# Forgetting attention: the output products of two heads issued together, alternating between the two column halves of the array

## The chip, the cores and the metric

The kernel runs on one core of a Trainium2 chip. The metric is the device time of one execution in microseconds (us), the median over several runs. TensorE (PE) multiplies, VectorE (DVE) and ScalarE (ACT) work on elements and move results out of the matmul banks (PSUM, banks of 128 partitions by 512 fp32 values), GpSimd (POOL) prepares weights, SyncE (SP) starts the loads. The engines run side by side, each in its own program order, and meet only at semaphores.

## The reference

Two blocks stand behind each other: a first block with a gated chunk mixer and a recurrent mixer, and a second with a feed-forward part, a hybrid mixer, a cross attention to a memory, and another feed-forward part. Sequence length is 512, width 1024, everything is fp32. The change touches the forgetting attention in the hybrid mixer:

```python
F = jnp.cumsum(jax.nn.log_sigmoid(f_logit.astype(jnp.float32)), axis=1).transpose(0, 2, 1)
...
s = jnp.einsum('bhqd,bshd->bhqs', q_blk, k, preferred_element_type=jnp.float32)
s = s + F_blk[..., None] - F[:, :, None, :]
s = jnp.where(pos_blk[:, None] >= k_pos[None, :], s, -jnp.inf)
p = jax.nn.softmax(s, axis=-1).astype(v.dtype)
return jnp.einsum('bhqs,bshd->bqhd', p, v)
```

There are 8 heads of 64 dimensions and 4 query tiles of 128 rows.

## The kernel before

**The stage.** The attention (`pe_fox`, `dve_fox`, `act_fox`, `pool_fox`) is a pipeline of `STEPS` = 32 steps: step i is head h = i // 4 and query tile qt = i % 4, and works on the first n = 128 (qt + 1) keys, since the attention is causal. Each engine has a loop over i that is unrolled in its own order. Beside the attention each step carries three of the 96 products of the convolution branch's projection (`pe_conv_products`: 9 matmuls of 128x512, L1679 to L1681), and that branch's elementwise work on DVE and ACT.

**One step on PE (iteration i).** First four matmuls that make the scores of step i (L1924 to L1927). Then the transposes of the softmax of step i - 2 (L1934, one for each key tile). Then, where a head begins (qt = 0) from i = 8 on, the output product `fox_out` of head h - 2 (L1953), so at i = 8, 12, 16, 20, 24, 28 and 32; the last head follows after the loop. Then the convolution products. After the 32 steps two more iterations (i = 32 and 33) carry the last transposes and 12 matmuls each of another projection (L1698 to L1700).

**The softmax.** For step i DVE takes the row maximum (L1978), ACT the exponential with its row sum (L2046), DVE the reciprocal (L1972), ACT multiplies by it (L2040, done in ACT's iteration i + 1). PE transposes the result (in its iteration i + 2), and ACT copies the transposed tile to SBUF (L2036, first thing in its iteration i + 3). ACT and DVE have other things in line between these: the taps of the convolution (L1719, up to three behind each other on DVE), L1709 that reads the projection's bank, L1737 and L1742 on ACT, and the preparation of the next head's queries, keys and rows (L1793, L1798, L1802 and L1816 on ACT, L1806 and L1810 on DVE).

**The output product.** The transposed softmax of a head lies in `FPT[:, h % 2]`, so there is a buffer for even heads and one for odd heads. `fox_out(pe, h)` waits for the four copies of head h (semaphore `fx_pt`) and makes four matmuls, one for each key tile, with 512, 384, 256 and 128 columns. The values of the head (128 keys by 64 dimensions) are the stationary operand. An even head writes partitions 0 to 63 of bank 4 and an odd head partitions 64 to 127; when both are there, ACT copies the bank (`act_fox_out`, L2070, semaphore `fx_oc`). ACT's first copy of a head h (step 4h) overwrites the buffer of head h - 2 and so waits for that head's output product (semaphore `fx_o`).

All operands of `fox_out` are plain fp32 (`FV` and `FPT`), and the trace has two matmul records for each such matmul of the program: 8 for a head, 64 for all.

Of the kernel before, what the change touches and what calls it, by code (L numbers as in the profile page):

```python
# [26 lines left out]
P = 128  # L27
SEQ = 512
TOK = SEQ // P
# [9 lines left out]
FOXH, FOXD = 8, 64  # L39
# [5 lines left out]
MH, MHD = 4, 256  # L45
# [89 lines left out]
def _members(kind, *parts):  # L135
# [21 lines left out]
    [("beta_tanh", 1), ("a_exp", 1), ("rows_exp", 1)],  # L157
    [("b_gates_lo", KB), ("causal", 2), ("masks", 26)], [("b_thg", KB), ("g_th", 4 * GH)], [("b_sg", KB), ("fx_r", FOXH * TOK)],
    [("raw_first0", 16), ("mem_in", 32)], [("raw_first1", 16), ("stored", 16 * KD)],
    [("fx_o", FOXH), ("ma_o", 2 * MH)], [("fx_hi", FOXH // 2), ("ma_hi", 2 * MH)], [("fx_lo", FOXH // 2), ("ma_lo", 2 * MH)],  # L160
]


class Sems:
# [18 lines left out]
    def due(self, name, value):  # L183

        return self(name), value + self.start.get(name, 0)
# [21 lines left out]
def build(nc, dram, out, phases=PHASES, dump=None):  # L207
# [3 lines left out]
    with ctx:  # L211
        base = 16640

        def place(name, at_kib, shape, dt=F32):
            return nc.alloc_sbuf_tensor_at(name, [P] + shape, dt, offset=base + int(at_kib * KIB))
# [22 lines left out]
        PS = [ctx.enter_context(nc.psum_tensor(f"bank{i}", [P, SEQ], F32))[:, :] for i in range(8)]  # L238

        S = Sems(nc, ctx)  # L240
        due = S.due
# [1310 lines left out]
        EVEN, ODD = slice(0, FOXD), slice(FOXD, P)  # L1552
        FV = place("fox_v_rows", YAT + 16, [TOK, SEQ])
# [15 lines left out]
        FPT = place("fox_pt", ZAT + 8, [2, TOK, SEQ])  # L1569
# [96 lines left out]
        def pe_conv_products(pe, i):  # L1666

            for c in range(3 * i, 3 * i + 3):
                t, k = divmod(c, KD)
                ph, r, side = mix_tile(t)  # L1670
                j, q = 2 * side + k // 4, k % 4
                if k == 0 and t == 0:
                    pe.wait_ge(*due("cols", 1))
                elif k == 0 and t >= 2:
                    pe.wait_ge(*due("g_xb", t - 1))
                if q == 0:
                    pe.wait_ge(units_ready, ph.used(r, j))
                wh, wl, ps = WH[:, SLOT[j] + q, :], WL[:, SLOT[j] + q, :], mix_bank(t)
                nc.tensor.matmul(ps, wh, XH[:, k, :], start=k == 0, stop=False)  # L1679
                nc.tensor.matmul(ps, wl, XH[:, k, :], start=False, stop=False)  # L1680
                last = nc.tensor.matmul(ps, wh, XL[:, k, :], start=False, stop=k == KD - 1)  # L1681
                if q == 3:
                    last.then_inc(units_used, 1)
# [104 lines left out]
        def key_rest_copied(h):  # L1788
            return 7 + h if h < 2 else 4 * h + 4
# [118 lines left out]
        def score_bank(i):  # L1908
            return PS[(0, 1, 7)[i % 3]]

        def pe_fox(pe):
            pe.wait_ge(*due("fk", PFQ.rounds))
            pe.wait_ge(*due("mask_b", 2))
            for i in range(STEPS + 2):
                h, qt = divmod(i, TOK)
                if i < STEPS:
                    if qt == 0:
                        pe.wait_ge(*due("fx_rowc", h + 1))
                        pe.wait_ge(*due("fx_rest", 2 * h + 2))
                        pe.wait_ge(*due("fx_rounded", key_rest_copied(h)))  # L1920
                    n, ps = (qt + 1) * P, score_bank(i)
                    if i >= 3:
                        pe.wait_ge(*due("fx_e", i - 2))
                    nc.tensor.matmul(ps[:, 0:n], F_SEL[:, h % 2, qt * P:n], F_K[:, 0:n], start=True, stop=False)  # L1924
                    nc.tensor.matmul(ps[:, n - P:n], IDENT_B[:, :], CAUSAL_B[:, :], start=False, stop=False)
                    nc.tensor.matmul(ps[:, 0:n], FX_Q[h % 2][:, qt * P:n], FX_K[h % 2][:, 0, 0:n], start=False, stop=False)
                    nc.tensor.matmul(ps[:, 0:n], FX_Q[h % 2][:, qt * P:n], FX_K[h % 2][:, 1, 0:n], start=False, stop=True).then_inc(S("fx_s"), 1)  # L1927
                j = i - 2
                if 0 <= j < STEPS:
                    pe.wait_ge(*due("fx_p", j + 1))  # L1930
                    if j >= 2:
                        pe.wait_ge(*due("fx_pt", j - 1))
                    for kt in range(j % TOK + 1):
                        last = nc.tensor.transpose(PS[2 + j % 2][:, kt * P:(kt + 1) * P], FP[:, j % 2, kt * P:(kt + 1) * P], IDENT[:, :])  # L1934
                    last.then_inc(S("fx_t"), 1)
                if i >= 8 and qt == 0:
                    fox_out(pe, h - 2)
                if i < STEPS:
                    pe_conv_products(pe, i)
                else:  # L1940
                    pe_mix_half(pe, NCONV, i - STEPS)
                if SUMS_FROM <= i < STEPS:
                    for n in range(2):
                        pe_square_sums(pe, 2 * (i - SUMS_FROM) + n)
            fox_out(pe, FOXH - 1)

        def fox_out(pe, h):
            pe.wait_ge(*due("fx_pt", TOK * (h + 1)))
            if h >= 2 and h % 2 == 0:
                pe.wait_ge(*due("fx_oc", h // 2))  # L1950
            half = slice(64 * (h % 2), 64 * (h % 2) + 64)
            for kt in range(TOK):
                last = nc.tensor.matmul(PS[4][half, kt * P:SEQ], FV[:, kt, h * FOXD:(h + 1) * FOXD], FPT[:, h % 2, kt, kt * P:SEQ],  # L1953
                                        start=kt == 0, stop=kt == TOK - 1)
            last.then_inc(S("fx_o"), 1)

        def dve_fox(dve, step):
# [68 lines left out]
        def act_fox(act):  # L2026
            MXC, SUMC = SC[:, 0:32], SC[:, 32:64]
            for i in range(STEPS + 3):
                h, qt = divmod(i, TOK)
                j = i - 3  # L2030
                if 0 <= j < STEPS:
                    jh, jq = divmod(j, TOK)
                    act.wait_ge(*due("fx_t", j + 1))
                    if jh >= 2 and jq == 0:
                        act.wait_ge(*due("fx_o", jh - 1))
                    nc.scalar.activation(FPT[:, jh % 2, 0:jq + 1, jq * P:(jq + 1) * P], PS[2 + j % 2][:, 0:(jq + 1) * P].rearrange("p (k q) -> p k q", q=P), ACT.Copy).then_inc(S("fx_pt"), 1)  # L2036
                if 1 <= i <= STEPS:
                    n = ((i - 1) % TOK + 1) * P
                    act.wait_ge(*due("fx_r", i))
                    nc.scalar.activation(FP[:, (i - 1) % 2, 0:n], FP[:, (i - 1) % 2, 0:n], ACT.Copy, scale=SUMC[:, i - 1:i]).then_inc(S("fx_p"), 1)  # L2040
                if i < STEPS:
                    n = (qt + 1) * P
                    act.wait_ge(*due("fx_nm", i + 1))
                    if i >= 2:
                        act.wait_ge(*due("fx_t", i - 1))
                    nc.scalar.activation(FP[:, i % 2, 0:n], score_bank(i)[:, 0:n], ACT.Exp, bias=MXC[:, i:i + 1], accum_out=SUMC[:, i:i + 1]).then_inc(S("fx_e"), 1)  # L2046
                started, ended = tile_at(i, 0), tile_at(i, 2)
                if ended is not None:
                    act_mix_end(act, ended)
                if started is not None:  # L2050
                    act_mix_start(act, started)
                if qt == 1 and h + 1 < FOXH:
                    act_head_rows(act, h + 1)
                if qt == 3 and h + 2 < FOXH:
                    act_round_query(act, h + 2)
                elif qt < 2 and 1 <= h and h + 1 < FOXH:
                    act_round_key(act, h + 1, qt)
                elif qt == 2 and 1 <= h and h + 1 < FOXH:
                    act_copy_key_rest(act, h + 1)
                if i >= 8 and qt == 2 and h % 2 == 1 and i < STEPS:  # L2060
                    act_fox_out(act, (h - 3) // 2)
                if SUMS_FROM - 1 <= i < SUMS_FROM + 1:
                    act_square(act, 2 * (i + 1 - SUMS_FROM))
                    act_square(act, 2 * (i + 1 - SUMS_FROM) + 1)
            act_fox_out(act, FOXH // 2 - 1)

        def act_fox_out(act, m):

            act.wait_ge(*due("fx_o", 2 * m + 2))
            nc.scalar.activation(FQ[:, m, :], PS[4], ACT.Copy).then_inc(S("fx_oc"), 1)  # L2070

        def act_fox_hi(act):
# [54 lines left out]
        def pe_square_sums(pe, j):  # L2127
            if j == 0:
                pe.wait_ge(*due("g_xb", NCONV - 1))
            square_sums(pe, j, T[:, 4 + j % 2, :])  # L2130
# [1002 lines left out]
```

## Time and profile before

| | |
|---|---|
| time, median of 3 runs | 1885.44 us (1885.00 to 1885.52) |
| span of the profiled execution, first to last instruction | 1882.1 us |
| time of the runs less that span | 3.3 us |
| PE busy | 1847.4 us, 98% of the span |
| DVE, ACT, POOL busy | 872.6, 518.6 and 1291.5 us |
| TensorE clock granted, mean | 0.996 |
| the stage, first scores to the end of the last output product | about 1061 to 1187.5 us |

The span is that of one profiled execution; the time of an execution also has what lies ahead of its first and behind its last instruction, so 3.3 us are added to a span to compare it with the runs. PE is busy nearly all of the time, but the records of matmuls overlap and their ends are modelled, so starts are read and not ends. The view of idle times says what an engine waited for; the chain of waits says which work the end of the program hangs on.

### The profile page before, as it was taken

The numbers are of one execution on the slowest core, as the hardware profiler recorded it, in microseconds if no ns is written. First come the engines' busy times: TensorE is split into PE (matmuls) and PEld (weight loads), VectorE is DVE, ScalarE is ACT, GpSimd is POOL, SyncE is SP. The second block draws the span as 40 slices with busy tenths as digits, with TensorE's granted clock in tenths as the row PEclk, the third lists the DMA queues.
The fourth block names the chain that finished last, engine by engine and source line by source line (L and its number), as shares of the span: only waits on it lengthen the run. The fifth ranks groups of instructions, "written<-read, shape, count | busy, mean of one in ns | idle before, by whom it ended". The sixth has DMA issues, their size and how long they took to land.

```text
span 1882.1 us, 25476 instructions
## 1 busy us (share of the span) xinstructions
PE 1847.4 (98%) x8692; PEld 1515.5 (81%) x8692; DVE 872.6 (46%) x1482; ACT 518.6 (28%) x950; POOL 1291.5 (69%) x1283
## 2 busy tenths in 40 slices
PE   7999999999999999999999999999999999999998
PEld 6888888878878788888888777798877778888886
DVE  5166663159963422234037666644364162222721
ACT  3111111147751111111033377343333231111001
POOL 7666667767777777776678754572772677777775
PEclk9999999999999999999999999999999999999999
DMA  4222224232222332232233211100331223223231
GB/s 182 99 82 90 88 89 146 99 115 78 81 84 101 112 109 92 89 120 106 86 112 101 72 63 45 46 24 1 134 113 45 70 78 110 89 90 111 90 112 68
DMA packets 25128, 170.45 MB, mean 91 GB/s; under 512 B 2784, under 2 KB 2912, under 8 KB 6624
## 3 DMA queue, kind: packets, MB, share of 16 engines
q1 hardware_dynamic: 23328, 159.92, 23.9%
q10 hardware_dynamic: 1728, 9.58, 1.4%
q8 instruction: 44, 0.72, 0.2%
q14 instruction: 28, 0.23, 0.0%
HBM read 167.39 MB, written 2.10 MB: 90 GB/s over the span
## 4 chain that ended last, share of the span: by engine, by line
PE 91%; DVE 4%; ACT 2%; POOL 2%; issue 1%; DMA 0%; DVEq 0%; POOLq 0%; ACTq 0%
PE bank L409 19%; PE bank L411 19%; PE bank L410 19%; PE bank L447 2%; PE bank L449 2%; PE bank L448 2%; PE bank L1292 2%; PE bank L1291 2%; PE bank L1290 2%; PE bank L2385 1%; PE bank L2369 1%; PE bank L1679 1%; POOL weights_lo L305 1%; PE bank L1953 1%; PE bank L1681 1%
## 5 line engine op out<-in xcount | busy, mean ns | idle before, releaser
L305 POOL TENSOR_TENSOR weights_lo<-raw_weights,weights_hi 128x512 fp32r<-128x512 f32 (+3 forms) x560 | 757.4, 1353 | 53.2 <-ACT weights_hi L324 7.2
L303 POOL TENSOR_SCALAR weights_hi<-raw_weights 128x512 fp32r<-128x512 f32 (+4 forms) x536 | 360.8, 673 | 422.6 <-PE bank L411 263.9
L409 PE MATMUL bank<-x_hi,weights_hi 128*128 128x512 f32 x1264 | 495.6, 392 | 0.3 <-POOL weights_lo L305 0.2
L411 PE MATMUL bank<-x_lo,weights_hi 128*128 128x512 f32 x1264 | 492.0, 389 | 0.0
L410 PE MATMUL bank<-x_hi,weights_lo 128*128 128x512 f32 x1264 | 491.9, 389 | 0.0
L409 PEld LDWEIGHTS bank<-x_hi,weights_hi 128*128 128x128 f32 x1264 | 237.3, 188 | 50.4 <-issue 1.7
L410 PEld LDWEIGHTS bank<-x_hi,weights_lo 128*128 128x128 f32 x1264 | 237.3, 188 | 49.7 <-issue 1.0
L411 PEld LDWEIGHTS bank<-x_lo,weights_hi 128*128 128x128 f32 x1264 | 237.2, 188 | 49.7
L1092 DVE TENSOR_TENSOR temps<-bank,rms_rows 128x512 f32<-128x512 f32 x44 | 30.4, 690 | 185.6 <-PE bank L411 185.6
L1082 ACT ACTIVATE ffn_y_hi<-temps 128x512 f32 (+1 forms) x44 | 27.8, 632 | 228.9 <-DVE temps L1095 228.9
L447 PE MATMUL bank<-weights_hi,x_hi 128*128 128x512 f32 x160 | 64.2, 401 | 10.2 <-DVE x_lo L557 9.7
L1080 ACT ACTIVATE temps<-temps 128x512 f32<-128x512 f32 x44 | 27.8, 632 | 159.1 <-DVE temps L1090 159.1
L1090 DVE TENSOR_TENSOR temps<-bank,rms_rows 128x512 f32<-128x512 f32 x44 | 30.4, 691 | 87.5 <-PE bank L411 84.9
L409 PE MATMUL bank<-ffn_y_hi,weights_hi 128*128 128x512 f32 x176 | 68.8, 391 | 0.0
L411 PE MATMUL bank<-ffn_y_lo,weights_hi 128*128 128x512 f32 x176 | 68.5, 389 | 0.0
L410 PE MATMUL bank<-ffn_y_hi,weights_lo 128*128 128x512 f32 x176 | 68.5, 389 | 0.0
L1290 PE MATMUL bank<-weights_hi,ffn_y_hi 128*128 128x512 f32 x176 | 68.5, 389 | 0.0
L1291 PE MATMUL bank<-weights_lo,ffn_y_hi 128*128 128x512 f32 x176 | 68.5, 389 | 0.0
L1292 PE MATMUL bank<-weights_hi,ffn_y_lo 128*128 128x512 f32 x176 | 68.5, 389 | 0.0
L449 PE MATMUL bank<-weights_hi,x_lo 128*128 128x512 f32 x160 | 62.8, 392 | 0.0
L448 PE MATMUL bank<-weights_lo,x_hi 128*128 128x512 f32 x160 | 62.8, 392 | 0.0
L1281 POOL TENSOR_TENSOR weights_lo<-raw_weights,weights_hi 128x512 fp32r<-128x512 f32 x44 | 57.2, 1300 | 3.7
(484 smaller groups left out, 3284.8 us busy)
## 6 DMA issues: line engine op xcount, KB each, us to landing
raw_weights<-in_ffn_up SPq DMA_DIRECT2D x44, 1024.0 KB, 4.8
raw_weights<-in_a_ug SPq DMA_DIRECT2D x16, 1024.0 KB, 4.7
raw_weights<-in_b_in SPq DMA_DIRECT2D x12, 1024.0 KB, 4.7
raw_weights<-in_ffn_down SPq DMA_DIRECT2D x8, 1408.0 KB, 6.1
raw_weights<-in_ffn_down SPq DMA_DIRECT2D x11, 1024.0 KB, 4.8
raw_weights<-in_a_out SPq DMA_DIRECT2D x8, 1024.0 KB, 4.8
raw_weights<-in_a_v SPq DMA_DIRECT2D x7, 1024.0 KB, 4.8
raw_weights<-in_b_out SPq DMA_DIRECT2D x8, 768.0 KB, 4.2
```

The lines of the kernel that those rows point to most:

```text
L303: nc.gpsimd.tensor_scalar(hi, raw, 1.0, 0.0, ALU.mult, ALU.add).then_inc(S("units_hi"), 1)
L305: nc.gpsimd.tensor_tensor(lo, raw, hi.bitcast(F32), ALU.subtract).then_inc(units_ready, 1)
L409: nc.tensor.matmul(ps, wh, xh[:, k, :], start=k == 0, stop=False)
L410: nc.tensor.matmul(ps, wl, xh[:, k, :], start=False, stop=False)
L411: last = nc.tensor.matmul(ps, wh, xl[:, k, :], start=False, stop=k == last_k)
L447: nc.tensor.matmul(bank, xh[:, k, tok], wh, start=k == 0, stop=False)
L448: nc.tensor.matmul(bank, xh[:, k, tok], wl, start=False, stop=False)
L449: last = nc.tensor.matmul(bank, xl[:, k, tok], wh, start=False, stop=k == KD - 1)
L1281: nc.gpsimd.tensor_tensor(lo, raw, hi.bitcast(F32), ALU.subtract).then_inc(units_ready, 1)
L1290: nc.tensor.matmul(bank, Y_H[:, k, tok], wh, start=k == 0, stop=False)
L1291: nc.tensor.matmul(bank, Y_H[:, k, tok], wl, start=False, stop=False)
L1292: return nc.tensor.matmul(bank, Y_L[:, k, tok], wh, start=False, stop=k == KF - 1)
```

## The change

`fox_out` is called four times and not eight. Each call waits for both heads of a pair and makes their eight matmuls in turn: key tile 0 of the even head, key tile 0 of the odd head, key tile 1 of the even head, and so on, so that neighbours write different halves of bank 4. The calls stand at the head of PE's iterations i = 11, 19 and 27, ahead of the scores of that step, and after the loop. ACT's first copy of an even head waits for the pair two heads back, and that of an odd head waits for nothing of the kind any more.

```diff
@@ pe_fox @@
             for i in range(STEPS + 2):
                 h, qt = divmod(i, TOK)
+                if i >= 11 and qt == 3 and h % 2 == 0:
+                    fox_out(pe, h // 2 - 1)
                 if i < STEPS:
...
                     last.then_inc(S("fx_t"), 1)
-                if i >= 8 and qt == 0:
-                    fox_out(pe, h - 2)
                 if i < STEPS:
                     pe_conv_products(pe, i)
...
-            fox_out(pe, FOXH - 1)
-
-        def fox_out(pe, h):
-            pe.wait_ge(*due("fx_pt", TOK * (h + 1)))
-            if h >= 2 and h % 2 == 0:
-                pe.wait_ge(*due("fx_oc", h // 2))
-            half = slice(64 * (h % 2), 64 * (h % 2) + 64)
+            fox_out(pe, FOXH // 2 - 1)
+
+        def fox_out(pe, m):
+
+            pe.wait_ge(*due("fx_pt", 2 * TOK * (m + 1)))
+            if m:
+                pe.wait_ge(*due("fx_oc", m))
             for kt in range(TOK):
-                last = nc.tensor.matmul(PS[4][half, kt * P:SEQ], FV[:, kt, h * FOXD:(h + 1) * FOXD], FPT[:, h % 2, kt, kt * P:SEQ],
-                                        start=kt == 0, stop=kt == TOK - 1)
+                for odd, half in enumerate((EVEN, ODD)):
+                    h = 2 * m + odd
+                    last = nc.tensor.matmul(PS[4][half, kt * P:SEQ], FV[:, kt, h * FOXD:(h + 1) * FOXD], FPT[:, odd, kt, kt * P:SEQ],
+                                            start=kt == 0, stop=kt == TOK - 1)
             last.then_inc(S("fx_o"), 1)
@@ act_fox @@
-                    if jh >= 2 and jq == 0:
-                        act.wait_ge(*due("fx_o", jh - 1))
+                    if jh >= 2 and jh % 2 == 0 and jq == 0:
+                        act.wait_ge(*due("fx_o", jh // 2))
@@ act_fox_out @@
-            act.wait_ge(*due("fx_o", 2 * m + 2))
+            act.wait_ge(*due("fx_o", m + 1))
```

On PE, before, this is iteration i = 8, from the scores of step 8 over the transposes of step 6 to the output product of head 0, and the first convolution products:

```order
L1924 MATMUL bank<-fox_f_rows,fox_f_selected 128x128 [waits fx_rounded,fx_e,fx_rest,fx_rowc]
L1925 MATMUL bank<-causal_b,ident_b 128x128
L1926 MATMUL bank<-fox_k_even,fox_q_even 128x128
L1927 MATMUL bank<-fox_k_even,fox_q_even 128x128
L1934 MATMUL bank<-ident,fox_p 128x128 [waits fx_pt,fx_p]
L1934 MATMUL bank<-ident,fox_p 128x128 x2
L1953 MATMUL bank<-fox_pt,fox_v_rows 64x512 [waits fx_pt]
L1953 MATMUL bank<-fox_pt,fox_v_rows 64x384
L1953 MATMUL bank<-fox_pt,fox_v_rows 64x256
L1953 MATMUL bank<-fox_pt,fox_v_rows 64x128
L1679 MATMUL bank<-x_hi,weights_hi 128x512 [waits units_ready,b_xb]
```

In the changed kernel (its lines stand two further down from here on) nothing of this kind stands in iteration 8. This is the seam between iterations 10 and 11 on PE:

```order
L1679 MATMUL bank<-x_hi,weights_hi 128x512 [waits units_ready,b_xb]
L1680 MATMUL bank<-x_hi,weights_lo 128x512
L1681 MATMUL bank<-x_lo,weights_hi 128x512
L1955 MATMUL bank<-fox_pt,fox_v_rows 64x512 [waits fx_pt]
L1955 MATMUL bank<-fox_pt,fox_v_rows 64x512
L1955 MATMUL bank<-fox_pt,fox_v_rows 64x384 x2
L1955 MATMUL bank<-fox_pt,fox_v_rows 64x256 x2
L1955 MATMUL bank<-fox_pt,fox_v_rows 64x128 x2
L1926 MATMUL bank<-fox_f_rows,fox_f_selected 128x512 [waits fx_e]
L1927 MATMUL bank<-causal_b,ident_b 128x128
L1928 MATMUL bank<-fox_k_even,fox_q_even 128x512
L1929 MATMUL bank<-fox_k_even,fox_q_even 128x512
```

The eight products of heads 0 and 1 now stand ahead of the scores of step 11, and the first of them carries the wait for head 1's last copy.

On ACT the order of the instructions is the same in both kernels, but the waits differ. This is where iteration 14 ends and iteration 15 begins (the copy L2038 is that of step 12, head 3), in the changed kernel:

```order
L1802 ACTIVATE fox_k_even<-fox_k_even 64x512 [waits fx_rest]
L2072 ACTIVATE fox_q<-bank 128x512 [waits fx_o]
L2038 ACTIVATE fox_pt<-bank 128x128 [waits fx_t]
L2042 ACTIVATE fox_p<-fox_p,scratch_cols 128x384 [waits b_sg]
L2048 ACTIVATE fox_p,scratch_cols<-bank,scratch_cols 128x512 [waits fx_t,fx_nm]
```

Before, that copy (L2036 there) waited for `fx_o` too; the copies of steps 8, 16 and 24 wait for it in both kernels, and in the changed kernel what they wait for stands in PE's iterations 11, 19 and 27.

## Rows read from the trace of the kernel before

**Rows 1.** Busy times in the stage, all engines
```profile
1061.00:1187.50 126.50, 124.59 (x616) 91.95 (x616) 85.69 (x157) 83.68 (x191) 69.28 (x79) 1.00 0.17 59
```

**Rows 2.** Waits in the stage: waiter, releaser, us in total, times, longest
```profile
POOL weights_hi L303 <- PE bank L1681: 47.9, 23, 5.3
...
DVE scratch_cols L1978 <- PE bank L1927: 12.3, 11, 1.9
```

**Rows 3.** Output products by form: busy us, mean ns of one
```profile
L1953 PE MATMUL bank<-fox_pt,fox_v_rows 128*64 128x512 f32 x16 | 8.6, 618 | 0.0
...
L1953 PE MATMUL bank<-fox_pt,fox_v_rows 128*64 128x128 f32 x16 | 3.1, 272 | 0.0
```

**Rows 4.** Timeline of PE, iterations 4, 15 and 16: start us, us, what
```profile
1072.16 0.22 PE L1924 MATMUL bank<-fox_f_rows,fox_f_selected 128*128 128x128 f32 x1
...
1074.95 0.28 PE L1924 MATMUL bank<-fox_f_rows,fox_f_selected 128*128 128x256 f32 x1
...
1111.89 0.39 PE L1924 MATMUL bank<-fox_f_rows,fox_f_selected 128*128 128x512 f32 x1
...
1115.02 0.22 PE L1924 MATMUL bank<-fox_f_rows,fox_f_selected 128*128 128x128 f32 x1
...
1115.83 2.37 PE L1953 MATMUL bank<-fox_pt,fox_v_rows 128*64 128x512 f32 x8
1118.13 0.50 PE L1679 MATMUL bank<-x_hi,weights_hi 128*128 128x512 f32 x1
...
1120.30 0.28 PE L1924 MATMUL bank<-fox_f_rows,fox_f_selected 128*128 128x256 f32 x1
```

**Rows 5.** Timelines of PE, ACT and DVE, iterations 10 to 13
```profile
1096.36 0.58 ACT L2036 ACTIVATE fox_pt<-bank 128x512 f32<-128x512 f32 x1
...
1100.16 0.25 ACT L2036 ACTIVATE fox_pt<-bank 128x128 f32<-128x128 f32 x1
...
1104.47 0.69 DVE L1806 TENSOR_TENSOR fox_q_even<-fox_q,fox_q_even 64x512 fp32r<-64x512 f32 x1
...
1106.05 0.28 PE L1924 MATMUL bank<-fox_f_rows,fox_f_selected 128*128 128x256 f32 x1
...
1106.73 0.43 DVE L1978 TENSOR_REDUCE scratch_cols<-bank 128x1 f32<-128x256 f32 x1 [1.57 <-PE bank L1927]
```

**Rows 6.** Timelines of ACT and DVE, from step 13's maximum to step 15's copy
```profile
1114.69 0.69 DVE L1978 TENSOR_REDUCE scratch_cols<-bank 128x1 f32<-128x512 f32 x1
...
1119.03 0.35 ACT L2046 ACTIVATE fox_p<-bank,scratch_cols 128x128 f32<-128x128 f32 x1
...
1122.53 0.41 DVE L1978 TENSOR_REDUCE scratch_cols<-bank 128x1 f32<-128x256 f32 x1
...
1125.24 0.57 ACT L2036 ACTIVATE fox_pt<-bank 128x512 f32<-128x512 f32 x1
```

**Rows 7.** Timeline of PE, from iteration 29 to the stage's end
```profile
1163.89 0.28 PE L1924 MATMUL bank<-fox_f_rows,fox_f_selected 128*128 128x256 f32 x1
...
1176.75 2.37 PE L1953 MATMUL bank<-fox_pt,fox_v_rows 128*64 128x512 f32 x8
...
1185.20 2.37 PE L1953 MATMUL bank<-fox_pt,fox_v_rows 128*64 128x512 f32 x8
1187.50 0.73 PE L1906 MATMUL bank<-gdn_split_rows,row_selectors 128*128 128x512 f32 x2
```

**Rows 8.** Timeline of PE in a later stage, two 64x64 products that meet
```profile
1275.39 0.94 PE L2406 MATMUL bank<-gdn_inv,gdn_l_t 64*64 64x64 f32 x13 [0.27 <-ACT temps L2434]
1276.11 0.27 PE L2414 MATMUL bank<-gdn_inv_t,temps 64*64 64x64 f32 x1
1276.17 0.22 PE L2406 MATMUL bank<-gdn_inv,gdn_l_t 64*64 64x64 f32 x1
1276.22 0.22 PE L2414 MATMUL bank<-gdn_inv_t,temps 64*64 64x64 f32 x1
1276.22 0.22 PE L2406 MATMUL bank<-gdn_inv,gdn_l_t 64*64 64x64 f32 x1
```

More of the change, by code:

```diff
@@ L159 @@
     [("raw_first0", 16), ("mem_in", 32)], [("raw_first1", 16), ("stored", 16 * KD)],
-    [("fx_o", FOXH), ("ma_o", 2 * MH)], [("fx_hi", FOXH // 2), ("ma_hi", 2 * MH)], [("fx_lo", FOXH // 2), ("ma_lo", 2 * MH)],
+    [("fx_o", FOXH // 2), ("ma_o", 2 * MH)], [("fx_hi", FOXH // 2), ("ma_hi", 2 * MH)], [("fx_lo", FOXH // 2), ("ma_lo", 2 * MH)],
 ]
```

## The prediction, made before the changed kernel was run

> **What bounds the kernel now.** I read the page first, then the busy times of the stage, its waits, and the timelines of PE, ACT and DVE against each other. In the stage PE is busy 124.59 of 126.50 us at a full clock of 1.00 [rows 1], so by shares alone every microsecond taken from PE is won. POOL, which feeds the weights, waits 47.9 us for PE [rows 2] and can follow a faster one. DVE and ACT are busy 85.69 and 83.68 us [rows 1], but each works in order and they form a loop, so shares say nothing about their slack. DVE waits for scores only 12.3 us in the whole stage, 11 times in 32 steps [rows 2]; elsewhere the scores wait for DVE. Between those waits ACT and DVE run a chain of their own. Step 13's maximum starts at 1106.73, having waited 1.57 us for PE [rows 5]. From there the queues of the two alternate: L1709 on DVE, L1737 and four more on ACT, step 14's exponential, its reciprocal and two taps on DVE, step 15's maximum at 1114.69, five items of ACT up to step 16's exponential at 1119.03, its reciprocal, three taps and L1806 on DVE, step 17's maximum at 1122.53, and through ACT again to the copy of step 15's tile at 1125.24, which ends at 1125.81 [rows 6]. None of these had to wait for PE: 1125.81 - 1106.73 = 19.08 us on which PE has no part. The pattern repeats every 8 steps, since three convolution tiles take 8.
>
> **The cost of the products.** A block of one head runs from 1115.83 to the next matmul at 1118.13, 2.30 us. Iteration 16 as a whole takes 5.28 us (1115.02 to 1120.30) and iteration 4, with the same shapes and no block, 2.79 (1072.16 to 1074.95) [rows 4]: a head costs 2.49 us, 0.19 of it ahead of the first product, and eight cost 19.9 us. A 512-column record lasts 618 ns and a 128-column one 272 [rows 3]: 0.90 ns a column, near two passes of 0.417 ns at 2.4 GHz. The 2 x 1280 columns of a head's eight records then stream in 2.13 us, and 0.17 us of the block is the seam behind it.
>
> **What a pair costs** (X, from its first product to the matmul behind it). The trace has no two 128x64 products side by side. Upper bound, one after the other: 2 x 2.13 + 0.17 = 4.43 us. Lower bound, fully side by side, like one head: 2.30 us. Between them, if starts keep the program's order: each fp32 product is two records in the same half, so the odd head's first record can start only with the even head's second, and X is one 512-column record longer, 2.30 + 0.43 = 2.73 us. The nearest row is that of two fp32 products of 64x64 in different quarters of the array. L2406 alone starts 13 records in about 0.72 us, 0.056 us each; where L2414 joins, a record of each starts at 1276.22, and one of L2414 starts at 1276.11, ahead of an L2406 record at 1276.17 that stands before it in the program [rows 8]. So two quarters work at once, in fp32, and not strictly in order. There rows and columns of the array differ, here only the columns. I take X = 2.40 us, near the lower end.
>
> The Trainium skill, TensorE: Matmul & The Clock Gate (Part 3, packing small matmuls), says that matmuls start and end strictly in the program's order. By that rule X would be 2.73 us; the starts at 1276.11 and 1276.17 in this trace don't agree with it. It becomes rival A.
>
> **What moves, and what it meets.** PE alone would win 8 x 2.49 - 4 x (2.40 + 0.19) = 9.6 us. I don't forecast that, since the chain of ACT and DVE stands in the way.
>
> *The loop.* Up to step 7's copy (1096.36 to 1096.94 [rows 5]) the maxima wait for DVE's own queue, so the block taken out of iteration 8 wins nothing by itself: PE merely reaches iteration 11 earlier. There the new block waits for that copy and starts at 1097.00 (0.06 us for the signal, my estimate). Queued behind this wait are the scores of steps 11 to 13, for which DVE waits. PE's path to step 13's maximum is then X = 2.40; iteration 11, 3.13 us (as 1111.89 to 1115.02); iteration 12, 2.79 us (as iteration 4) [rows 4]; and 0.68 us from iteration 13's start to the maximum (1106.05 to 1106.73 [rows 5]). Sum 9.00, so 1106.00 in place of 1106.73: 0.73 us won. DVE would be free for it at 1104.47 + 0.69 = 1105.16, so PE sets it.
>
> ACT's copy of step 8 now waits for the block's end, 1099.4; before it started at 1100.16 [rows 5], so the wait is covered by 0.8 us. From step 13's maximum the 19.08 us run as before, and step 15's copy is what the next block (i = 19) waits for. PE gets there early: iterations 13 to 18 hold 5.84 us (1106.05 to 1111.89) + 5.92 + 5.84 = 17.6 us of work [rows 4, 5], against 0.68 + 19.08 = 19.76. Each of the three blocks in the loop thus gives 0.73 us: **2.2 us**.
>
> *The end.* Between step 29's scores (1163.89) and 1187.50 PE shows no wait [rows 7]. One block of 2.49 us goes (1176.75), and the last becomes a pair, 2.30 - 2.40 = -0.10. ACT mostly waits for PE there. **2.4 us.**
>
> *Behind it.* The stage after begins on PE with inputs that have long been there. No DMA and no instruction of POOL moves past another. The copies on ACT keep their order; odd heads lose a wait that never bound. All of this costs nothing. Sum 4.6 us: the span from 1882.1 to 1877.5, and with the 3.3 us around it 1880.8.
>
> **Rivals.** As a function of X the sum is 3 (3.13 - X) + 4.79 - X = 14.18 - 4X.
>
> A, starts in order, X = 2.73: 3.3 us, 1882.1. The skill's rule aside, the order within one half speaks for it, rows 8 against.
>
> B, the halves don't overlap at all, X = 4.43: the block ends at 1101.4, past the 1100.16 at which ACT wants to copy, and step 13's maximum comes at 1097.00 + 4.43 + 6.60 = 1108.03, 1.3 us later than before, three times; the end wins 4.79 - 4.43. **Slower** by 3.5 us, 1888.9. From X = 3.5 on there is a loss. Against it speak the quarters [rows 8]; for it, that both halves take all 128 rows of the array, which no row shows at once.
>
> C, the chain of ACT and DVE gives way too. PE's own 9.6 us would be 1875.8. But all that DVE leaves in a period is 1106.00 - 1105.16 = 0.84 us, so three times that and no more as I read the queues: 7.1 us, 1878.3.
>
> D, the gain is eaten: PE now idles 1 to 2 us ahead of each block, which could bring the granted clock down from 1.00, or a later stage keeps its time by its weights. Then no change, 1885.4, or a little over.
>
> **How the numbers follow.** The forecast (X from 2.30 to 2.59) has 0.50, A 0.20, B 0.14, C 0.08, D 0.08. 0.2% is 3.8 us, about what runs of this kernel can tell from no change. Faster by more takes X under 2.60: nearly all of the forecast and C, 0.53 with the edge of A taken against what a wrong microsecond loses. Within it: A, most of D, half of B, 0.37. Slower: half of B and a little of D, 0.10. The forecast's own range is 1880.0 to 1881.9. With A, C and D it reaches from 1878.3 to 1886.0, which leaves out B and a tail beyond C, under 2 in 10.
>
> **What would show it.** In the changed trace a pair's products should take 2.3 to 2.6 us from the first start to the next line; 4.4 means B. PE should idle 1 to 2 us ahead of the blocks in iterations 11, 19 and 27, released by ACT's copy. Step 13's maximum should come 9.1 us behind the end of step 7's copy (before, 9.8), and from it to the end of step 15's copy there should still be 19 us. If that is shorter, I misread the chain, and the gain is larger. PE should be 4.6 us ahead at the stage's end and still so at the end of the program; if the first holds and the second not, a later stage ate it.

## The result, and the profile after

| | before | changed |
|---|---|---|
| median of 20 runs | 1884.94 us (1884.18 to 1885.52) | 1888.16 us (1885.32 to 1888.56) |
| ratio | | 1.0015, 95% interval 1.0009 to 1.0021 |
| span of the profiled execution | 1882.1 us | 1886.6 us |
| mean granted clock | 0.996 | 0.993 |

The change makes the kernel 3.2 us slower; 4.6 us less were forecast. The profiled span is 4.5 us longer, but 1.04 us of that lies ahead of the stage: its first scores start at 1062.10 and not 1061.06. From there to the first matmul behind the stage it is 129.97 us (1192.07 less 1062.10) in place of 126.44 (1187.50 less 1061.06 [rows 7]): 3.5 us, which is the difference of the medians and a little more. The loss lies in the stage. (The 3.3 us between the runs and the span of before hold for that one profiled execution. Of the profiled execution of the changed kernel the time is known too, 1888.36 us, 1.8 above its span of 1886.6. So stages are compared by their length within a trace, and kernels by their medians.)

The timeline of PE in the changed kernel, at the block of iteration 11 and at the last block behind the loop (start, us, what, and idle time with its releaser):

```profile
1096.20 0.40 PE L1681 MATMUL bank<-x_lo,weights_hi 128*128 128x512 f32 x1
1098.89 4.06 PE L1955 MATMUL bank<-fox_pt,fox_v_rows 128*64 128x512 f32 x16 [2.29 <-ACT fox_pt L2038]
1102.89 0.50 PE L1926 MATMUL bank<-fox_f_rows,fox_f_selected 128*128 128x512 f32 x1
...
1189.76 2.38 PE L1955 MATMUL bank<-fox_pt,fox_v_rows 128*64 128x512 f32 x16
1192.07 0.73 PE L1906 MATMUL bank<-gdn_split_rows,row_selectors 128*128 128x512 f32 x2
```

From their first start to the next matmul the same 16 records take 2.31 us at the end (1189.76 to 1192.07), as one head did (2.30 [rows 4]), and 4.00 us (1098.89 to 1102.89) in the loop. The blocks of iterations 19 and 27 read like that of 11: 1129.92 to 1133.92 and 1161.03 to 1164.89. What sets them apart is the clock. Busy times by stretch (span, us, then PE, PEld, DVE, ACT, POOL busy, granted clock, DMA share and GB/s), in the whole block of iteration 11 and in the part of it in which the clock was down:

```profile
1098.90:1102.90 4.00, 4.00 (x17) 1.67 (x17) 1.66 (x4) 2.38 (x5) 0.00 (x0) 0.57 0.78 264
1099.36:1102.77 3.41, 3.41 (x16) 1.47 (x12) 1.23 (x3) 1.92 (x5) 0.00 (x0) 0.50 0.77 291
```

For 3.41 us the clock stands at 0.50, the lower of its two levels (1.2 of 2.4 GHz), and half of that, 1.70 us, is what the block takes longer. The same happened at the other two blocks of the loop, from 1130.08 to 1133.49 and from 1160.80 to 1164.21; before, the clock stood at 1.00 throughout the stage [rows 1]. PE had been idle for 2.29, 2.34 and 2.31 us ahead of the three blocks. The fall comes 0.47 and 0.16 us behind the start of the first two and 0.23 us ahead of the third. Of the 20 runs, 4 lie at 1885.3 to 1885.8 with a mean clock of 0.996 or 0.997, the 16 others at 1888.0 to 1888.6 with 0.993 to 0.995. The clock seems not to fall each time, though these 4 weren't profiled: they are some 2.7 us faster, less than the three falls are worth (4.9, see below).

The second thing is on DVE. POOL's and DVE's timelines ahead of the block of iteration 19:

```profile
1123.57 0.87 POOL L303 TENSOR_SCALAR weights_hi<-raw_weights 128x512 fp32r<-128x512 f32 x1 [2.00 <-PE bank L1681]
1124.52 1.60 POOL L305 TENSOR_TENSOR weights_lo<-raw_weights,weights_hi 128x512 fp32r<-128x512 f32 x1
1125.01 1.67 DVE L1806 TENSOR_TENSOR fox_q_odd<-fox_q,fox_q_odd 64x512 fp32r<-64x512 f32 x1
1126.60 0.41 DVE L1980 TENSOR_REDUCE scratch_cols<-bank 128x1 f32<-128x256 f32 x1
```

L1806 takes 1.67 us. It starts inside POOL's subtraction and ends at 1126.68, 0.56 us behind it (1124.52 + 1.60 = 1126.12), as if it had waited for it. Before, the same instruction took 0.69 us and was over when POOL's subtraction started, at 1123.18:

```profile
1121.92 0.69 DVE L1806 TENSOR_TENSOR fox_q_odd<-fox_q,fox_q_odd 64x512 fp32r<-64x512 f32 x1
```

Counted from step 13's maximum, POOL's subtraction comes 14.93 us behind it in the changed kernel and came 16.45 us behind it before. Step 17's maximum waits behind L1806 in DVE's order, and step 15's copy on ACT comes 2.70 us behind that maximum, as before (2.71). L1810 runs behind step 17's maximum; it takes 1.66 us in place of 1.25 and delays step 18's maximum, but not step 15's copy. The waits in the stage, to be read beside [rows 2]:

```profile
POOL weights_hi L303 <- PE bank L1681: 54.1, 22, 8.5
...
DVE scratch_cols L1980 <- PE bank L1929: 19.0, 14, 3.3
...
PE bank L1955 <- ACT fox_pt L2038: 6.9, 3, 2.3
```

DVE waits 19.0 us for scores in place of 12.3, and the last row is new: PE waits at the three blocks for ACT's copy.

### The profile page after: what moved, and what is told of

It is laid out like the page before. It is cut to its first block, busy times and chain, and to the rows that moved or that the text cites. A ratio compares the mean times of both kernels' runs of the same rounds, so it can differ in the third digit from the quotient of the medians.

```text
span 1886.6 us, 25473 instructions
## 1 busy us (share of the span) xinstructions
PE 1842.0 (98%) x8692; PEld 1513.3 (80%) x8692; DVE 877.0 (46%) x1482; ACT 519.4 (28%) x950; POOL 1290.2 (68%) x1283
## 4 chain that ended last, share of the span: by engine, by line
PE 89%; DVE 4%; ACT 3%; POOL 2%; issue 1%; DMA 0%; DVEq 0%; POOLq 0%; ACTq 0%
PE bank L409 19%; PE bank L411 19%; PE bank L410 19%; PE bank L447 2%; PE bank L449 2%; PE bank L448 2%; PE bank L1292 2%; PE bank L1291 2%; PE bank L1290 2%; PE bank L2387 1%; PE bank L2371 1%; POOL weights_lo L305 1%; PE bank L2535 1%; PE bank L686 1%; PE bank L2537 1%
```

## The experiments

A period is 8 steps, from one block's start in the loop to the next (before, from the end of step 7's copy to that of step 15's: 28.87 us). Beside the first four kernels the kernel before took 1884.96 us, beside the next four 1884.78 and beside the last two 1884.95; what is called faster than before below goes by these. A gain over the changed kernel goes by its 1888.16 us. The low parts in some of them are what POOL's subtraction writes, `weights_lo`.

**The heads in turn.** The even head's four products, then the odd head's.

```diff
-            for kt in range(TOK):
-                for odd, half in enumerate((EVEN, ODD)):
+            for odd, half in enumerate((EVEN, ODD)):
+                for kt in range(TOK):
```

> The changed kernel, with the four products of the even head ahead of the four of the odd head, at the same places. Theory 1 (the halves do overlap; the loop's blocks took 4.0 us and not 2.4 because the granted clock stood at half for 3.41 us from their start): a pair streams 4.27 us at full clock, of which 3.41 us at half do 1.71, so a block in the loop takes 3.41 + 2.56 + 0.17 = 6.1 us, 2.1 more than now, and the last pair 4.4 in place of 2.38. In all 3 x 2.1 + 2.05 = 8.4 us slower than the changed kernel, 1896.5. Theory 2 (no overlap in the loop, 4.0 us is simply two heads one behind the other at full clock): the loop's blocks stay at 4.0 and only the last grows, 1890.2.

Measured: 1891.10 us, 2.9 more than the changed kernel. The first two blocks of the loop and the last one behind it:

```profile
1099.82 3.93 PE L1955 MATMUL bank<-fox_pt,fox_v_rows 128*64 128x512 f32 x16 [2.31 <-ACT fox_pt L2038]
1130.71 5.60 PE L1955 MATMUL bank<-fox_pt,fox_v_rows 128*64 128x512 f32 x16 [2.33 <-ACT fox_pt L2038]
...
1192.04 3.93 PE L1955 MATMUL bank<-fox_pt,fox_v_rows 128*64 128x512 f32 x16
```

and the clock (third number from the end) in the first two:

```profile
1099.80:1103.70 3.90, 3.88 (x17) 1.83 (x17) 1.67 (x4) 2.41 (x5) 0.00 (x0) 1.00 0.76 271
1130.70:1136.20 5.50, 5.49 (x16) 2.30 (x16) 1.64 (x4) 2.40 (x5) 0.00 (x0) 0.69 0.00 0
```

The third block, at 1163.32, reads like the first. In the profiled execution the clock fell in one block of three, though PE had idled as long ahead of each (2.31, 2.33 and 2.34 us). From first start to the next matmul a pair in turn takes 3.86 us at full clock against 2.31 alternating: the alternation is worth 1.55 us. It is 3.86 and not twice 2.30, since the odd head starts before the even one is through: its first record, of 512 columns, starts at 1101.38, beside one of the even head's of 256 columns at 1101.37 and ahead of the even head's last three (1101.59, 1101.80 and 1101.91).

Both theories missed the time. Theory 1's 1896.5 had the pair in turn 0.57 us too long, four times, and took three falls of the clock for granted where this execution had one; together these come to 5.7 us, and 5.4 were missed. The two blocks of 3.9 us at full clock are what theory 2 expected, but not the one of 5.5 at 0.69. So this run alone doesn't decide; the next one does.

**The idle time filled.**

```diff
-            pe.wait_ge(*due("fx_pt", 2 * TOK * (m + 1)))
             if m:
                 pe.wait_ge(*due("fx_oc", m))
+            if m < FOXH // 2 - 1:
+                for _ in range(2):
+                    nc.tensor.matmul(PS[4], FV[:, 0, 0:P], FV[:, 0, :], start=True, stop=True)
+            pe.wait_ge(*due("fx_pt", 2 * TOK * (m + 1)))
```

> The changed kernel, with two fp32 products of 128x128 by 128x512 (about 0.85 us each, their result is overwritten) ahead of the wait for the copies in the three blocks of the loop, so that PE's idle time there goes from 2.3 to about 0.6 us. Theory 1 (the idle time brings the granted clock down): the clock stays at 1.00 in the loop, the blocks take 2.4 us, and 3 x 1.6 = 4.8 us are won over the changed kernel, 1883.4, in all runs alike. Theory 2 (no overlap in the loop): blocks stay at 4.0 us, 1888.2. Theory 3 (a neighbour such as ACT's traffic slows the block): also 1888.2, with the clock at 1.00.

Measured: 1882.77 us, ratio to before 0.9989 (0.9980 to 0.9998), 5.4 us faster than the changed kernel. Filling products and block of iteration 19:

```profile
1125.67 1.88 PE L1953 MATMUL bank<-fox_v_rows 128*128 128x512 f32 x4
1128.16 2.37 PE L1958 MATMUL bank<-fox_pt,fox_v_rows 128*64 128x512 f32 x16 [0.62 <-ACT fox_pt L2041]
```

All four blocks take 2.37 us (2.30 or 2.31 to the next matmul) at a clock of 1.00, with ACT's copies beside them as in the changed kernel. Theory 1 holds, and 2 and 3 fall: the idle time ahead of the block is what lets the clock fall. But the period is 29.34 us (1098.82 to 1128.16), still longer than the 28.87 of before: L1806 and L1810 take 1.67 us here too. The stage is 1.5 us shorter than before (124.94 against 126.44 us), and its end alone wins 2.5.

**The blocks behind the transposes** of the same iterations.

```diff
-                if i >= 11 and qt == 3 and h % 2 == 0:
-                    fox_out(pe, h // 2 - 1)
...
                     last.then_inc(S("fx_t"), 1)
+                if i >= 11 and qt == 3 and h % 2 == 0:
+                    fox_out(pe, h // 2 - 1)
                 if i < STEPS:
                     pe_conv_products(pe, i)
```

> The changed kernel, with the three blocks of the loop moved behind the scores and transposes of the same iterations (11, 19, 27). The idle time is then cut in two by about 1 us of scores. Theory 1: if the clock holds, blocks take 2.4 us, the scores of step 11 are early, ACT's copy of step 8 can start about 1 us earlier than now, and step 13's maximum comes 1.8 us earlier each time: 5.4 us, 1882.8. If the clock still falls, most of the 1.6 us is lost again and about 1887 is left. Theory 2 (no overlap): 1888 or a little less.

Measured: 1887.99 us. PE idles 2.03 us ahead of the transposes, the clock falls all the same in all three blocks, and they take 3.5 to 3.8 us. That is the case of a clock that still falls, and 1 us more than its 1887. Two of the 11 runs took 1884.7 and 1884.9 us.

**Only the last pair joined**, on the kernel before.

```diff
-                if i >= 8 and qt == 0:
+                if i >= 8 and qt == 0 and h < FOXH:
                     fox_out(pe, h - 2)
...
-            fox_out(pe, FOXH - 1)
+            for kt in range(TOK):
+                for h, half in ((FOXH - 2, EVEN), (FOXH - 1, ODD)):
...
```

> The kernel before, with heads 6 and 7 alone joined behind the loop (the block of head 6 in iteration 32 goes, heads 0 to 5 stay as they were). By the term of the prediction for the end, 2.49 us less and a pair of 2.38 in place of 2.30: 2.4 us faster than before, 1882.5. If a later stage ate what is won at the stage's end, 1884.9.

Measured: 1882.36 us, ratio 0.9987 (0.9978 to 0.9996): 2.6 us faster than before, 2.4 forecast; the stage is 2.46 us shorter. The gain at the stage's end reaches the program's end.

**Hardly a product in the loop.**

```diff
-            for kt in range(TOK):
+            for kt in range(TOK if m == FOXH // 2 - 1 else 0):
...
+            if m < FOXH // 2 - 1:
+                last = nc.tensor.matmul(PS[4][EVEN, 384:SEQ], FV[:, 3, 0:FOXD], FPT[:, 0, 3, 384:SEQ], start=True, stop=True)
```

> The changed kernel, with the three blocks of the loop cut from eight matmuls to one of 64x128 (the outputs of heads 0 to 5 are left out but for that; waits and signals stay). It shows what ACT and DVE's chain takes with hardly a product in it. If that chain bounds the loop, as the prediction has it, a period of 8 steps (block start to block start) stays well above PE's own 24.0 us: 20.3 us from step 13's maximum to step 15's copy as in the changed kernel and 8.2 for the way from step 7's copy to step 13's maximum on DVE alone, 28.5 us in place of 31.0, 7.6 us faster than the changed kernel, 1880.5. If PE bounds it and the chain is elastic (rival C), a period near 26 us and 1873.

Measured: 1881.36 us. With the block down to 0.43 us a period still takes 28.99 us (1098.68 to 1127.67) and then 28.39. From the end of step 7's copy to step 13's maximum it is 8.70 us, and 8.88 and 8.68 in the later periods; rival C had reckoned with 8.22. So ACT's and DVE's chain holds the loop, not PE's work, and rival C falls. (The clock fell in two of the three places here as well.)

**Light subtraction on POOL**, in the changed kernel.

```diff
+            if ph.name == "gdn_qkv":
+                lo, raw, hi = lo[:, :, 0:8], raw[:, :, 0:8], hi[:, :, 0:8]
             nc.gpsimd.tensor_tensor(lo, raw, hi.bitcast(F32), ALU.subtract).then_inc(units_ready, 1)
```

> The changed kernel, with POOL's subtraction for the low parts of the loop's weights cut to 8 of 128 columns in each tile (the low parts of the rest are left out, so values differ). In the changed kernel two of DVE's subtractions of 64x512 per period (L1806, L1810) take 1.67 us each where before they took 0.69 to 1.25, at the same time as POOL's 1.60 us ones. If POOL's instruction holds DVE's up, they go back to 0.69, step 13's maximum to step 15's copy from 20.3 to 19.1 us or less, and 3 x 1.2 + 0.9 = 4.5 us are won, 1883.7. If DVE is slow for another reason, they stay at 1.67 and the time at 1888.2.

Measured: 1877.49 us, ratio to before 0.9962 (0.9949 to 0.9975), 10.7 us faster than the changed kernel and not 4.5. DVE, POOL and PE ahead of iteration 19's block:

```profile
1119.32 0.69 DVE L1808 TENSOR_TENSOR fox_q_odd<-fox_q,fox_q_odd 64x512 fp32r<-64x512 f32 x1
...
1121.17 0.69 DVE L1812 TENSOR_TENSOR fox_k_odd<-fox_k,fox_k_odd 64x512 fp32r<-64x512 f32 x1
...
1122.43 0.25 POOL L307 TENSOR_TENSOR weights_lo<-raw_weights,weights_hi 128x32 fp32r<-128x32 f32 x1
...
1123.27 2.37 PE L1957 MATMUL bank<-fox_pt,fox_v_rows 128*64 128x512 f32 x16 [1.33 <-ACT fox_pt L2040]
```

The subtractions are back at 0.69 us, so POOL's instruction had held them up. With that PE's idle time ahead of this block shrinks from 2.34 to 1.33 us, the clock stays at 1.00 in the loop, and the block takes 2.37 us. The collision had caused part of the idle time, and with it the fall of the clock: that is most of the missing part of the gain, 4.9 of the 6.2 us. A period is 27.70 us.

The collision had a second place that neither the prediction nor the expectation saw. The two taps ahead of step 15's maximum (two SBUF inputs each) took 2.45 us before, beside a subtraction of POOL's at 1112.15, and take 1.52 here:

```profile
1112.32 2.45 DVE L1719 SCALAR_TENSOR_TENSOR temps<-gdn_xb_a,vecs,temps 128x512 f32<-128x512 f32 x2
...
1110.17 1.52 DVE L1721 SCALAR_TENSOR_TENSOR temps<-gdn_xb_a,vecs,temps 128x512 f32<-128x512 f32 x2
```

The first line is from the kernel before, the second from this one. In the changed kernel they take 2.44 us, so this 0.9 us stood in the 19.08 us chain all along, and the change brought only L1806's.

**Both edits.**

> Both edits together: two products that fill PE's idle time ahead of the three blocks (clock stays up), and POOL's light subtraction. With the clock and the collision both out of the way the prediction's own arithmetic for the loop should hold: a period of about 28.1 us, a block of 2.4. The two edits then add: 5.4 us (measured for the first) and 4.5 us, 1878.3. If they don't add, something else than these two fills the period.

Measured: 1879.19 us, 1.7 more than with the light subtraction alone. The edits don't add: with the light subtraction the clock stays up anyway, so the filling has nothing left to win, and it costs. The filling products end later than step 7's copy (1096.89), the block starts at 1097.26, and a period is 28.01 us. The clock stayed up and the blocks took 2.38 us.

**The convolution products first**, as useful filling.

```diff
-                if i >= 11 and qt == 3 and h % 2 == 0:
+                if i >= 11 and qt == 3 and h % 2 == 0 and i < STEPS:
+                    pe_conv_products(pe, i)
                     fox_out(pe, h // 2 - 1)
...
                 if i < STEPS:
-                    pe_conv_products(pe, i)
+                    if not (i >= 11 and qt == 3 and h % 2 == 0):
+                        pe_conv_products(pe, i)
```

> A version meant to be used: the changed kernel with the convolution products of iterations 11, 19 and 27 ahead of the block and the scores, so that work that is needed anyway fills PE's idle time (2.1 us for 2.3). The clock should stay up and the block take 2.4 us. The way from step 7's copy to step 13's maximum loses 2.1 us of PE's work, 6.9 in place of 9.0, so that DVE sets it (8.2). Against the kernel with filling products a period is 0.8 to 1.0 us shorter, 2.7 us in all, 1880.1. If the clock falls all the same, 1885.

Measured: 1879.01 us, ratio to before 0.9970 (0.9957 to 0.9982). The block of iteration 19:

```profile
1127.80 2.38 PE L1957 MATMUL bank<-fox_pt,fox_v_rows 128*64 128x512 f32 x16 [0.27 <-ACT fox_pt L2040]
1130.11 0.51 PE L1927 MATMUL bank<-fox_f_rows,fox_f_selected 128*128 128x512 f32 x1
```

PE idles 0.27 us, the clock is 1.00 in the block, and the period is 27.96 us (1099.84 to 1127.80), although L1806 and L1810 still take up to 1.7 us. This version leaves nothing out and is 5.8 us faster than before, 9.2 faster than the change as made.

**The control: POOL's light subtraction on the kernel before.**

> The kernel before with POOL's light subtraction in the loop (low parts of 8 of 128 columns, the rest left out), the control for the same edit on the changed kernel. If the collision of POOL's and DVE's subtractions is mainly something that the change brought (PE frees the weights earlier, so POOL's work falls on L1806 and L1810), little is won here: one subtraction of 1.25 us goes back to 0.69 each period, some waits of PE of 0.25 to 0.5 us go, and PE stays the bound at 28.5 us a period: about 1.5 us, 1883.3, and the changed kernel with the same edit (1877.5) is 5.8 us ahead of it. If the collision costs before as much as after, 1880.

Measured: 1883.11 us, 1.8 us faster than before. Its period is 28.5 us, PE's own work as forecast. The same edit gives 1.8 us there and 10.7 in the changed kernel. That doesn't show that the collision is the change's own: from step 13's maximum to the end of step 15's copy it is 18.40 us here in place of 19.08, with the two taps at 1.52 us, so 0.7 us of it stood in the kernel before. There PE bounds the loop and hides it; in the changed kernel the chain bounds the loop, and its 20.28 us become 18.64. Some 1.0 of these 1.64 us are new with the change, about what L1806 lost.

**The convolution products first, with the light subtraction.**

> The version with the convolution products ahead of the block, with POOL's light subtraction. With neither collision nor idle clock the loop should be bound by ACT and DVE's chain alone: 19.1 or (as in the changed kernel with that edit) 18.7 us from step 13's maximum to step 15's copy, plus 8.3 from step 7's copy to step 13's maximum, a period of 27.0 to 27.4 us against 27.96 without the edit and 27.70 in the changed kernel with it; about 1876.0. If DVE was the bound between copy and maximum because of the collision only, PE's 6.9 us there show and the period is 26.

Measured: 1874.84 us, 10.1 us faster than before. A period is 27.42 us, the upper end of what the chain was expected to need, but by other parts: 18.52 us from step 13's maximum to the end of step 15's copy, and 8.89 from the end of step 7's copy to step 13's maximum. The time is 1.2 us lower than expected.

## Why the prediction was wrong, point by point

**What a pair costs** was right: X = 2.40 forecast, 2.30 or 2.31 measured, from the first product to the matmul behind it, at the end and in every block of the loop at full clock. That is the lower bound, a pair for the price of one head. The halves overlap in fp32, and rivals A (2.73) and B (4.43) fall; one behind the other is 3.86 and not 4.43 us, as the seam between the heads overlaps too. The time alone would have misled: 1888.16 us lies next to rival B's 1888.9, by another cause.

**The end** was right: 2.4 us forecast; from step 29's maximum to the stage's end it is 20.47 us (1171.60 to 1192.07) in place of 22.93, so 2.46, and 2.6 in the experiment that has this part alone.

**The loop** was wrong: +0.73 us won each time by the forecast; the period went from 28.87 to 31.03 us, 2.16 lost. Two steps failed:

- "PE's path to step 13's maximum is then X = 2.40". That took the block at full clock. The idle time ahead of it was forecast as 1 to 2 us (by the prediction's own 19.76 less 17.6 it is 2.2) and was 2.3; that the clock might fall stood as rival D, with 0.08 and a time, 1885.4 "or a little over", that wasn't worked out from any row. The clock fell, and the blocks took 4.00, 4.00 and 3.86 us. From the end of the copy ahead of it to the maximum behind it (steps 7 and 13, then 15 and 21, 23 and 29) it was 10.75, 10.75 and 10.63 us where 9.06 were forecast: 4.9 us. With the clock at 1.00 (light POOL) the way from the block's start to step 13's maximum was 9.00 us (1095.57 to 1104.57), the forecast sum to the hundredth. That is luck in part: the block took 2.30 us for 2.40 and iteration 11 3.22 us for 3.13.
- "From step 13's maximum the 19.08 us run as before." They ran 20.28 (1109.59 to 1129.87), 1.2 us more, twice between the three blocks; and step 7's copy came 0.86 us later behind the first scores than before. I had counted POOL as an engine with slack. "No DMA and no instruction of POOL moves past another" is true, but "costs nothing" doesn't follow from it: PE frees the weights at other times, POOL's subtractions follow, and they fall on DVE's. L1806 takes 0.98 us more in these 1.2; the 0.25 us by which the three taps ahead of it are longer stay with light POOL, and their cause is open. With light POOL the chain is 18.64 us (1104.57 to 1123.21), less than the 19.08 forecast, since the collision of the two taps in it goes too.

These add to 4.95 + 2.40 + 0.86 = 8.2 us, less 0.1 by which the end did better: 8.1 us, the distance between 4.6 us won and 3.5 us lost at the stage's end. The two are not independent: the collision lengthens the wait that lets the clock fall. Whether DVE's subtraction waits for POOL's is shown by taking POOL's away. The Trainium skill, SBUF — State Buffer (Who interferes with whom), says that a DVE instruction with two SBUF inputs contends with a GpSimd instruction that reads SBUF and that the later one is blocked; the 1.67 us against 0.69, and the end 0.56 us behind POOL's, agree with it, and so do the taps' 2.45 us against 1.52. It stood there to be used in the forecast.

**Rival C** was rightly small: with hardly a product in it the loop still needs 28.4 to 29.0 us. **Rival D** named one of the two causes, the fall of the clock.

What stays open: why the clock fell at some blocks and not at others with the same 2.3 us of idle time ahead. No run varied that alone.

## What to carry to other kernels

Two products of 64 output columns that alternate between the halves of the array cost one and not two here, in plain fp32 (2.31 us for two heads, 2.30 for one); but to bring them side by side both must be ready, and the wait for the later one falls on PE. Put work that is needed anyway ahead of such a wait: it turned this change from 3.2 us slower than before to 5.8 us faster. And when PE's order changes, look at what it releases: an engine with slack, like POOL here, can still hit another one at the wrong moment.

## What the runs showed of the hardware

- Behind 2.29, 2.34 and 2.31 us of idle time on PE the granted clock stood at half for 3.41 us each time in the profiled execution of the change, and so it did behind 2.03 us with the blocks behind the transposes. With the heads in turn it fell at one of three blocks with 2.3 us ahead. With 1.33, 0.62 or 0.27 us ahead of the block it stayed at 1.00 in the loop.
- A subtraction of 64x512 on DVE took 1.67 us and not 0.69 beside POOL's of 128x512, and two taps of 128x512 took 2.45 us and not 1.52.
- 16 fp32 records for two halves took 2.31 us alternating and 3.86 in turn to the next matmul, at full clock. Alternating, the two heads' first records start 0.01 us apart; in turn, the second head's first record starts ahead of the first head's last three.
